# A gated expert product in two passes over column halves: one wide product for high and low gate parts, the low parts made by GpSimd

## What is computed

```
act = gelu(einsum('tkd,td->tk', u, xb))       # u, v: rows of the 16384 chosen experts
y   = einsum('tk,tkd->td', gb * act, v)       # gb: gates of the chosen experts
out = rmsnorm(x + y, final_norm_gain)
```

## Time and profile before

| | |
|---|---|
| median of 3 runs | 1999.95 us (1996.71 to 2000.69) |
| the profiled execution's own time | 1985.34 us |
| its span, first to last instruction | 1983.5 us |
| TensorE busy | 1955.4 us, 99% of the span |
| VectorE, ScalarE, GpSimd busy | 1326.7, 911.6, 1361.0 us |
| mean granted TensorE clock | 0.997 |
| read from memory | 445 MB, 227 GB/s over the span |

### The profile page before, as it was taken

One profiled execution on the slowest core, in us unless ns is written; L12 is line 12 of the kernel. 1 busy time (PEld: TensorE's weight loads), 2 busy tenths in 40 slices (PEclk: granted clock), 3 DMA queues, 4 the chain that ended last, 5 costly groups with the idle time before them and its releaser, 6 DMA issues.

```text
span 1983.5 us, 38782 instructions
## 1 busy us (share of the span) xinstructions
PE 1955.4 (99%) x13920; PEld 1843.1 (93%) x13920; DVE 1326.7 (67%) x2423; ACT 911.6 (46%) x1198; POOL 1361.0 (69%) x704
## 2 busy tenths in 40 slices
PE   8999999999999999999999999999999999999997
PEld 6888888888999999999999999999999999999997
DVE  6544683155536778778888886257888867777865
ACT  6453354474444444544444444433444444444443
POOL 7866768877888999988888888807555514444400
PEclk9999999999999999999999999999999999999998
DMA  8645656555765666666666666779999979999863
GB/s 326 191 138 151 200 149 223 182 179 161 228 186 181 206 207 209 198 199 192 191 193 196 191 191 192 246 247 330 328 328 322 333 239 316 304 306 310 308 198 115
DMA packets 126109, 450.69 MB, mean 227 GB/s; under 512 B 16464, under 2 KB 17104, under 8 KB 124880
## 3 DMA queue, kind: packets, MB, share of 16 engines
q1 hardware_dynamic: 101520, 365.76, 58.1%
q0 software_dynamic: 20480, 67.13, 9.7%
q10 hardware_dynamic: 4032, 16.76, 2.3%
HBM read 445.39 MB, written 4.19 MB: 227 GB/s over the span
## 4 chain that ended last, share of the span: by engine, by line
PE 56%; POOL 31%; issue 12%; DVE 1%; POOLq 0%; DMA 0%; ACT 0%; DVEq 0%
POOL wlo L404 30%; PE ps L1707 13%; PE ps L1785 11%; PE ps L1786 11%; PE ps L1787 11%; PE ps L1709 6%; PE ps L1720 1%; PE ps L1819 0%; POOLq L403 0%; PE ps L1860 0%; DVE big L1407 0%; DMA x_back<-in_u_rows,big 0%; POOL x_back L420 0%; POOLq L407 0%; DVE big L1398 0%
## 5 line engine op out<-in xcount | busy, mean ns | idle before, releaser
L404 POOL TENSOR_TENSOR wlo<-raw,whi 128x1024 fp32r<-128x1024 f32 x444 | 1077.2, 2432 | 206.0 <-ACT whi L466 189.9
L466 ACT ACTIVATE whi<-raw 128x1024 fp32r<-128x1024 f32 x436 | 461.7, 1060 | 637.8 <-PE ps L1709 361.3
L1707 PE MATMUL ps<-x_parts,whi 128*128 128x448 f32 x2048 | 654.6, 376 | 1.3 <-POOL wlo L404 1.3
L1785 PE MATMUL ps<-gate_hi,whi 128*128 128x224 f32 x2048 | 563.5, 275 | 3.9 <-DVE wlo L1310 2.3
L1786 PE MATMUL ps<-gate_lo,whi 128*128 128x224 f32 x2048 | 563.2, 275 | 0.0
L1787 PE MATMUL ps<-gate_hi,wlo 128*128 128x224 f32 x2048 | 563.1, 275 | 0.0
L1709 PE MATMUL ps<-x_parts,wlo 128*128 128x224 f32 x2048 | 540.8, 264 | 0.0
L638 ACT ACTIVATE whi<-raw 128x1024 fp32r<-128x1024 f32 x256 | 271.7, 1061 | 386.2 <-PE ps L1787 374.3
L1707 PEld LDWEIGHTS ps<-x_parts,whi 128*128 128x128 f32 x2048 | 384.6, 188 | 34.4 <-ACT big L592 1.1
L1310 DVE TENSOR_TENSOR wlo<-raw,whi 128x1024 fp32r<-128x1024 f32 x248 | 303.9, 1226 | 160.5 <-ACT whi L638 160.0
L1785 PEld LDWEIGHTS ps<-gate_hi,whi 128*128 128x128 f32 x2048 | 393.7, 192 | 4.3 <-DVE wlo L1310 2.5
(11 more groups left out here) (242 smaller groups left out, 2298.5 us busy)
## 6 DMA issues: line engine op xcount, KB each, us to landing
raw<-in_w_u SPq DMA_DIRECT2D x256, 512.0 KB, 3.5
raw<-in_w_v SPq DMA_DIRECT2D x256, 512.0 KB, 4.7
raw<-in_w_front SPq DMA_DIRECT2D x180, 512.0 KB, 3.6
big<-in_x_t ACTq DMA_DIRECT2D x4, 512.0 KB, 9.4
big<-in_x ACTq DMA_DIRECT2D x4, 512.0 KB, 7.3
big<-in_mem ACTq DMA_DIRECT2D x4, 512.0 KB, 7.1
big<-in_mem_t ACTq DMA_DIRECT2D x2, 1024.0 KB, 6.1
big<-in_x ACTq DMA_DIRECT2D x2, 1024.0 KB, 6.7
```

Of the source, the lines that this page charges most:

```text
L404: nc.gpsimd.tensor_tensor(wlo[:, j % SPL, :], raw[:, j % RAW, :], whi[:, j % SPL, :], ALU.subtract).then_inc(lo_done, 1)
L466: nc.scalar.activation(whi[:, j % SPL, :], raw[:, j % RAW, :], ACT.Copy).then_inc(hi_done, 1)
L1707: nc.tensor.matmul(sums[:, 0:2 * TD], whi[:, s, cols], x_parts[:, :, m, 0:TD], start=m == 0, stop=False, skip_group_check=True)
L1785: nc.tensor.matmul(out, whi[:, s, cols], gate_hi[:, g, 0:TD], start=opens, stop=False, skip_group_check=True)
```

## The change

The pieces of V come in another order: first the lower half of the columns for all 128 chunks, then the upper half. So only 8 column blocks are open at a time, one to a bank, and a block's high-weight product takes both gate parts in one matmul of 448 columns into two halves of the bank (`v_block`), as in stage U. At the turn between the halves (pieces 127 and 128) VectorE adds the two halves of each bank into `FIRST` (`first_block`), and TensorE's first product of the second half waits block by block for that (`first_joined`). In the second half VectorE squares `FIRST` one block in every 12 pieces, and ScalarE multiplies it by the gain in the last four pieces. After the last piece VectorE joins the 8 blocks of the second half into `SECOND`, ScalarE squares them, and TensorE sums 9 products (one for all of the first half). The output is multiplied in three shares: 8 blocks by VectorE, 5 by GpSimd, 3 by VectorE in one instruction.

Each chunk's gate parts are now made twice, once for each piece. ScalarE makes the high part for every piece; VectorE makes the low part for the first 8 pieces alone, and GpSimd makes it for the other 248 (`gate_rest`). TensorE waits for `glo_pool_done` before each piece. GpSimd's gathers stand between these in one written order: the ring is now 12 single rows, the plan takes 50 rows of U in 41 pieces and 25 rows of V in 21 pieces. The residual comes in two loads and two groups of products, after pieces 23 and 131.

```diff
-GROUPS = P // 4
+RING = 12
 ACT_BANKS = 3
 POOL_END = V0 + 8
 FOLD_BODY, LAST_ROWS = 10, 242
+OPENING, SPARE_BLOCKS = 8, 5
+
+
+def issued_u(d):
+    return OPENING + d // 2 if d < RING else taken_u(d - RING) + 1
+
+
+def taken_u(d):
+    return 14 + d * 41 // 50
+
+
+def issued_v(e):
+    return 116 + e * 3 // 4 if e < 8 else 135 + (e - 8) // 2 if e < 12 else 137 + (e - 12) * 21 // 25
+
+
+def taken_v(e):
+    return 132 + e * 4 // 5 if e < 8 else 140 + (e - 8) * 21 // 25
...
-        gate_hi = sb("gate_hi", [P, 2, T], F32R)
-        gate_lo = sb("gate_lo", [P, 2, T], F32R)
-        sb("rest_of_gates", [P, 576])
+        gate_parts = sb("gate_parts", [P, SPL, 2, TD], F32R)
+        sb("rest_of_gates", [P, 256])
...
-        x2_back = sb("x2_back", [P, TB, D])
+        x2_back = sb("x2_back", [P, 2, TB, PW])
...
+        FOURS = [gather_low[:, 0], gather_low[:, 1], x2_back[:, 1].rearrange("p a (b c) -> p (a b) c", c=PD)]
+        ROW = [FOURS[k // 4][:, k % 4, :] for k in range(RING)]
+        FIRST = x2_back[:, 0].rearrange("p a b -> p (a b)")[:, 0:8 * TD].rearrange("p (a b) -> p a b", a=8)
+        SUM_SQ, ONE_SQ = (at(TK_AT + 4 * PD + k * TD, TD) for k in range(2))
...
+            for ready, count, m0, m1 in ((y_out, 1, 8, 12), (y_first, 1, 0, SPARE_BLOCKS), (y_out, 2, 12, 16), (y_out, 3, SPARE_BLOCKS, 8)):
+                sp.wait_ge(ready, count)
+                sp.dma_start(out[:, m0:m1, :], OUT[:, m0:m1, :]).then_inc(out_done, 16)
             sp.wait_ge(out_done, 80)
...
+            def gate_rest(j):
+
+                pool.wait_ge(ghi_done, j + 1)
+                nc.gpsimd.tensor_tensor(gate_parts[:, j % SPL, 1, :], W[:, j % NK, :], gate_parts[:, j % SPL, 0, :],
+                                        ALU.subtract).then_inc(glo_pool_done, 1)
+
...
+            def gather_u(d):
+
+                if d >= RING:
+                    pool.wait_ge(rows_taken, d - RING + 1)
+                gather(d % RING, u_rows, IDX[0][:, d:d + 1])
+
+            def gather_v(e):
+
+                if e < 8:
+                    pool.wait_ge(rows_taken, P // RING * RING + e + 1)
+                if e == 8:
+                    pool.wait_ge(residual_in, 2)
+                if e >= RING:
+                    pool.wait_ge(rows_taken, P + e - RING + 1)
+                gather(e % RING, v_rows, IDX[1][:, e:e + 1])
+
+            asked = [0, 0]
+            for j in range(OPENING, 2 * NK):
+                gate_rest(j)
+                if j == OPENING:
+                    pool.wait_ge(picks, 1)
+                    pool.wait_ge(used, V0)
+                while asked[0] < P and j >= issued_u(asked[0]):
+                    gather_u(asked[0])
+                    asked[0] += 1
+                while asked[1] < P and j >= issued_v(asked[1]):
+                    gather_v(asked[1])
+                    asked[1] += 1
...
+            pool.wait_ge(first_gained, 8)
+            pool.wait_ge(last_root_ready, 1)
+            for m in range(SPARE_BLOCKS):
+                ins = nc.gpsimd.tensor_tensor(OUT[:, m, :], FIRST[:, m, :], LAST_R, ALU.mult)
+            ins.then_inc(y_first, 1)
...
-            def gated_high(k0, k):
-                nc.scalar.activation(gate_hi[:, k % 2, 0:TD], W[:, k0 + k, :], ACT.Copy).then_inc(ghi_done, 1)
+            def gated_high(k0, j):
+                nc.scalar.activation(gate_parts[:, j % SPL, 0, :], W[:, k0 + j, :], ACT.Copy).then_inc(ghi_done, 1)
...
+            gated_high(0, 2)
+
+            def load_back(h, tb):
+                act.dma_start(x2_back[:, h, tb, :], x2_dram[tb * P:(tb + 1) * P, h * PW:(h + 1) * PW]).then_inc(x2_in, 16)
...
+                if j in (3, 4):
+                    load_back(1, j - 3)
...
+                gated_high(-NK, j)
+                for c in range((j % RAW) * 2, (j % RAW) * 2 + 2):
+                    act.wait_ge(first_squared, c + 1)
+                    nc.scalar.activation(FIRST[:, c, :], FIRST[:, c, :], ACT.Copy, scale=GAIN[:, 5, c:c + 1]).then_inc(first_gained, 1)
...
+            act.wait_ge(glo_pool_done, 2 * NK - OPENING)
+            for c in range(8):
+                act.wait_ge(second_joined, c + 1)
+                nc.scalar.activation(SQ[:, c, :], SECOND[:, c, :], ACT.Square).then_inc(sq_act, 1)
...
             def u_row(slot):
-                row = gathered(0, slot)
+                dve.wait_ge(row_in[slot % RING], 16 * (slot // RING + 1))
+                row = ROW[slot % RING]
                 nc.vector.tensor_tensor_reduce(row, row, X_GAINED, 1.0, 0.0, ALU.mult, ALU.add,
                                                SUMS[:, slot:slot + 1]).then_inc(rows_taken, 1)
 
...
+            def joined_block(c, to, done):
+                nc.vector.reduce_sum(to[:, c, :], ps[:, c, 0:2 * TD].rearrange("p (h t) -> p t h", h=2), AX).then_inc(done, 1)
+
+            def first_block(c):
+                if c < 7:
+                    dve.wait_ge(block_done, c + 1)
+                else:
+                    dve.wait_ge(used, V0 + NK)
+                joined_block(c, FIRST, first_joined)
+
...
+            for j in range(2, 2 * NK):
+                if j == NK + 1:
+                    first_block(0)
+                    first_block(1)
...
+                if j == NK + 1:
+                    for c in range(2, 8):
+                        first_block(c)
+                if j > NK + BODY and j % BODY == 0 and j // BODY - FOLD_BODY - 2 < 8:
+                    square_first(j // BODY - FOLD_BODY - 2)
...
-                while done[0] < P and j >= (14 if done[0] < 8 else 20) + done[0] * 3 // 4:
+                while done[0] < P and j >= taken_u(done[0]):
...
-                while done[1] < P and j >= FOLD_BODY * BODY + 7 + done[1] * 7 // 8:
+                while done[1] < P and j >= taken_v(done[1]):
...
+            for c in range(8):
+                dve.wait_ge(block_done, 7 + c + 1)
+                joined_block(c, SECOND, second_joined)
...
+            nc.vector.tensor_tensor(LAST_R, LAST_R, LAST_T, ALU.mult).then_inc(last_root_ready, 1)
+            dve.wait_ge(last_root_ready, 1)
+            for k in range(2):
+                for c in range(4 * k, 4 * k + 4):
+                    ins = nc.vector.scalar_tensor_tensor(OUT[:, 8 + c, :], SECOND[:, c, :], GAIN[:, 5, 8 + c:9 + c], LAST_R,
+                                                         ALU.mult, ALU.mult)
                 ins.then_inc(y_out, 1)
+            dve.wait_ge(first_gained, 8)
+            rest = slice(SPARE_BLOCKS, 8)
+            nc.vector.tensor_tensor(OUT[:, rest, :], FIRST[:, rest, :],
+                                    LAST_R.unsqueeze(1).broadcast_to([P, 8 - SPARE_BLOCKS, TD]), ALU.mult).then_inc(y_out, 1)
...
+            def v_block(s, c, first=False, last=False):
+
+                cols = slice(c * P, (c + 1) * P)
+                g = (s - V0) % SPL
+                nc.tensor.matmul(ps[:, c, 0:2 * TD], whi[:, s, cols], gate_parts[:, g].rearrange("p k t -> p (k t)"),
+                                 start=first, stop=False, skip_group_check=True)
+                return nc.tensor.matmul(ps[:, c, TD:2 * TD], wlo[:, s, cols], gate_parts[:, g, 0, :],
+                                        start=False, stop=last, skip_group_check=True)
+
+            def v_ready(n0, j):
+                if isinstance(n0, int) and n0 + j < OPENING:
+                    pe.wait_ge(glo_done, n0 + j + 1)
                     pe.wait_ge(lo_done, V0 + j + 1)
                 else:
+                    pe.wait_ge(glo_pool_done, n0 + (j + 1 - OPENING))
                     pe.wait_ge(lo_v_done, n0 + (V0 - POOL_END + j + 1))
...
+
+            def v_piece(n0, j):
+                v_ready(n0, j)
+                for c in range(8):
+                    ins = v_block((V0 + j) % SPL, c)
                 ins.then_inc(used, 1)
+
+            def residual(h):
+                pe.wait_ge(x2_in, 32 * (h + 1))
+                for c in range(8):
+                    for tb, w in ((0, P), (1, TD - P)):
+                        ins = nc.tensor.matmul(ps[:, c, tb * P:tb * P + w], x2_back[:, h, tb, c * P:(c + 1) * P], ident[:, 0:w],
+                                               start=False, stop=False, skip_group_check=True)
+                ins.then_inc(residual_in, 1)
...
+            for c in (2, 3, 4, 5, 6, 7, 0, 1):
+                if c == 0:
+                    pe.wait_ge(act_taken, NK)
+                ins = v_block(V0 % SPL, c, first=True)
+            ins.then_inc(used, 1)
...
+                v_ready(FOLD_BODY * BODY, j)
+                for c in range(8):
+                    if j > last_first:
+                        pe.wait_ge(first_joined, c + 1)
+                    ins = v_block((V0 + j) % SPL, c, first=j > last_first, last=j == last_first)
+                    if j == last_first and c < 7:
+                        ins.then_inc(block_done, 1)
+                ins.then_inc(used, 1)
+            residual(1)
...
+            pe.wait_ge(second_joined, 1)
```

(67 more changed lines are left out.)

143 lines of the change are left out of this document (46 added, 97 removed).

## The result

| | before | changed kernel |
|---|---|---|
| median of 5 runs, first comparison | 1999.95 us (1996.71 to 2000.69) | 2010.54 us (2008.01 to 2016.53) |
| ratio | | 1.0059 [1.0041, 1.0078] |
| span of the profiled execution | 1983.5 us | 2014.7 us |
| start of the last product of stage V | 1964.4 us | 1997.8 us |

The change makes the kernel 0.6% slower; the forecast was 1973 us, and 2010.5 us also lies above the range for 8 in 10 (up to 2004). On a chip of the experiments the ratio is 1.0137 [1.0121, 1.0154]: the changed kernel takes 2011.6 us there, nearly as in the first comparison, and the kernel before only 1983.8 us, as on the two other chips of the experiments within 1 us. The trace of before (1985.3 us) was at that level. What kept the kernel before at 2000 us in the first comparison stays open; I count the terms by the experiments' chips.

What follows compares the result with a forecast made beforehand. Stage V was taken as bound by TensorE's matmul pace; -35.3 + 10 + 2 - 2.3 + 1 + 1.4 - 3.1 - 0.7 = -27.0 us, from 1999.95 to 1973 us. Own range 1965 to 1985; 8 in 10, 1959 to 2004.

Steps and rivals of the forecast that it cites:

- TensorE, -35.3 us: Stage V: the wide product takes each of 256 pieces from 2.673 to 2.535 us, 35.3 us less.
- GpSimd, +12 us: Stage V: low gate parts ahead of gathers cost 10 us over U's gathers and 2 us over V's.
- My 2.63 us: GpSimd's forecast time per piece with gathers of U in stage V, against TensorE's 2.535 us.
- So rows stretch a gather and `wlo` does not: GpSimd's gathers in V: claimed VectorE's row operations lengthen them, 1.13 us against 0.94 alone, and `wlo` doesn't.
- VectorE and ScalarE, 0: Stage V: VectorE's 2.39 or 2.50 us a piece and ScalarE's 1.06 + 0.37 fit under 2.535 us, no cost.
- Opening, -2.3 + 1 us: Start of V: the late-row stall of 2.3 us goes; low parts taking turns and 12 gathers on 6 pieces add 1.
- Turn, +1.4 us: Piece 128: VectorE's joins of 8 banks end at 6.4 us, not 5.07, so TensorE loses 1.4 us.
- End, -3.1 - 0.7 us: After the last piece: joins, square and one product save 3.1 us; the output saves 0.7 us.
- B: Rival, chance 0.17: GpSimd and VectorE exclude each other until GpSimd bounds V; 2015 us, decided from a 2.72 us mean.
- a late GpSimd no longer meets the start of `wlo`: Rival B's limit in stage V: only half the excess of 3.7 us over 2.63 allowed, so 3.2 us at most.
- A: Rival, chance 0.25: the cover holds everywhere in V, without GpSimd's 12 us and the opening's 1 us; -40 us, 1960 us.
- C: Rival, chance 0.10: transfers bound stage V at 2.59 us a piece, costing 10 us in place of 12; 1971 us.

Runs made afterwards that it cites:

- low_on_dve: Changed kernel with only the low gate parts taken back from GpSimd, so VectorE makes them all: 1939.44 us, ratio 0.9777 to before.
- low_on_dve_narrow: Changed kernel with all low gate parts on VectorE and three 224-column products to a block in place of the wide product: 1978.64 us, ratio 0.9977 to before.
- after_again: The changed kernel, unchanged, timed again on a chip of the experiments: 2011.58 us, ratio 1.0137 to before.
- narrow: Changed kernel, GpSimd's low gate parts kept, with three 224-column products to a block in place of the wide product: 2018.6 us, ratio 1.0174 to before.
- gate_high_first: Changed kernel with ScalarE making the high gate part before the high weight part, in all pieces but the first 12: 2002.33 us, ratio 1.0096 to before.

## Why the prediction was wrong

**TensorE, -35.3 us.** Right in mechanism, a little small: -39.2 us where nothing but TensorE bounds (low_on_dve less low_on_dve_narrow), or 256 x (2.673 - 2.520). The 12.04 us for 38 blocks gave 2.535 us, the windows above 2.52.

**GpSimd, +12 us.** The term that failed: it is +72.1 us (after_again less low_on_dve). My 2.63 us were 1.00 for the low part with its wait, 1.40 for the gathers and 0.23 for the gaps; measured were 0.90, 1.74 and 0.23 (1320 to 1560 us). For the gathers of V my 2.50 were 1.00, 1.28 and 0.22; 1700 to 1900 us has 1.05, 1.70 and 0.21, together 2.96. Against the pace of 2.52, 105 x 0.35 + 97 x 0.44 = 79 us, more or less the 76 us by which stage V is longer than in low_on_dve (1997.8 against 1922.0, both from 1266.2). The price of the unseen operation, 0.7 us, was right (0.69 us alone). The known operation was wrong.

The step that failed was "So rows stretch a gather and `wlo` does not". I took it from one gather under `wlo`, that of 1546.74. But `wlo` began at 1547.13, 0.39 us after it, too late to count by the rule above. By the same rule put to all 256 gathers of the kernel before, 155 began under an operation of VectorE (143 of them within 0.05 us of the rule), and 101 of these under `wlo`, with a median of 1.13 us; those under none, 101 too, took 0.945. The mean of 1.13 us was then a mean over phases, mostly those of `wlo`, and I carried it to a kernel in which the phase is another. As I read the runs, I left out two things. The gathers now follow the gate parts piece by piece, at the pace at which ScalarE hands them over: low_on_dve, without a low part on GpSimd, has 199 of its 256 gathers begin under `wlo`, with a mean of 1.37 us over all. And GpSimd's low part holds `wlo` back and so keeps more of it over the gather: of those under `wlo` the median is 1.77 us for 1.53, though fewer meet it, and the mean over all goes to 1.43. The first makes up most of the added stretch (1.11 to 1.37 of 1.43 us), though no run separates it from low_on_dve's faster pace. It became a loss because the low part's own 0.69 us and more no longer found room beside it.

**VectorE and ScalarE, 0.** VectorE in low_on_dve does more than I had priced for the change, and has every piece in time. In the changed kernel it is slowed (`wlo` 1.40 us in the mean for 1.23), but it is GpSimd that TensorE waits for. ScalarE's part was right.

**Opening, -2.3 + 1 us.** The stall of the earlier trace rows is gone in every version. The other part was 3.5 us of waits for GpSimd up to 1320 us in the changed kernel, and none in low_on_dve.

**Turn, +1.4 us.** 0.4 us, the one wait of low_on_dve. My order of the joins was right: two before `wlo`, six behind it. The first began at 1591.38 and the six took 3.27 us.

**End, -3.1 - 0.7 us.** From the last piece to the root it is 3.6 us for 6.3: -2.7. From the first output block to the end of the span it is 9.2 us for 8.7, so +0.5: I had priced VectorE's blocks without GpSimd beside them. All these small terms together were forecast at -3.7 us and are -5.2.

**The sum.** On the experiments' chips the forecast change was -27.0 and is +27.7 us: 60 for GpSimd, -4 for TensorE, -1.5 for the rest, 54.7 together. The split goes by way of low_on_dve; by way of narrow, where TensorE is slower, GpSimd's part would be 40.0 us and TensorE's -7.0.

**The rivals.** B came true in sign and place. Its mechanism was half right: the two engines do exclude each other, but the low part waits less than B said (0.87 and 1.03 us in the mean, 0.69 alone, so 0.18 and 0.34 us for 0.8). The gathers pay more, some 0.58 us to a piece over the 0.95 us that one takes alone. I had bounded B by "a late GpSimd no longer meets the start of `wlo`". That bound is wrong twice: of the 84 low parts from 1320 to 1560 us, 46 still begin under `wlo` (1.02 us in the mean, the others 0.68), and where one begins ahead of `wlo`, it makes `wlo` meet the gather. Its deciding point of 2.72 us in the mean was passed (2.87 and 2.96). A, the cover that holds everywhere, is low_on_dve: -44.4 us where it said -40. C is refuted: 335 GB/s at a share of 0.95, with no wait of TensorE (ScalarE's waits for `raw` are 12.4 us in all in low_on_dve, and hidden).

Whether GpSimd's low parts could be hidden by another written plan of the gathers, which keeps them clear of `wlo`, wasn't tried. Nor was low_on_dve run with gathers that don't wait for the gate parts, which would show how much of their stretch the plan itself makes. The version that beats both kernels is low_on_dve, 1939.4 us, 2.2% under the kernel before and 3.6% under the changed one.

## What to carry to other kernels

Before an engine gets new work, look at what its known operations cost by the phase in which they start, not by their mean: a mean hides which neighbour stretched them, and new work and a new order both move the phase. Don't conclude "this neighbour doesn't disturb" from an overlap of two bars; ask which of them was running at the moment when the other needed the shared resource, and put the reading to all instances in the trace. Where two engines hold each other up, as here, idle time of the one is not free: the small operation took 0.38 us on VectorE and was hidden there, and 0.69 us or more on GpSimd, where the kernel is 72 us slower with it.

## What the runs showed that I had not expected

- A gather's issue on GpSimd takes 0.94 to 0.96 us by itself and 1.77 us in the median when it begins under `wlo` in the changed kernel, up to 2.00 us; most end 0.82 to 0.83 us after the operation of VectorE with two SBUF inputs that they began under. Row operations of 2 columns in place of 512 made no difference to the kernel's time; a `wlo` of 32 columns took 71 us off.
- Less work on VectorE made gathers longer (1.57 us for 1.43), since more of them then began under `wlo` (194 of 256, beside 115).
- Two engines that hold each other up can fall into step: low part, `wlo`, gather, at 2.62 us. 57 steps of the changed kernel are within 0.05 us of this, and 60 of gate_high_first, where ScalarE worked in the other order.
- A TensorE pass with a 448-column and a 224-column product runs at 0.315 us for a block, three products of 224 columns at 0.334.
